# A conditioned transformer trunk: condition products in column strips, and the residual affine on GpSimd moved into the expert loop

## The reference, cut to what matters

```python
c_act = jax.nn.silu(c)
ada = c_act @ w_ada[l] + b_ada[l]                      # 1 x 6144
sh1, sc1, g1, sh2, sc2, g2 = jnp.split(ada, 6, axis=-1)
h = x * (1.0 + sc1) + sh1
m = pool mixer (layer 0) or sliding window attention (layer 1) of h
x = layernorm(ALPHA * x + g1 * m) * ln_g[l, 0] + ln_b[l, 0]
h = x * (1.0 + sc2) + sh2
f = moe(h)                                             # router, top 4, softmax, experts
x = layernorm(ALPHA * x + g2 * f) * ln_g[l, 1] + ln_b[l, 1]
```

## Time and profile before

| | us |
|---|---|
| median of three runs | 1534.92 |
| the profiled execution, its span | 1535.1 |
| end of the mixing in the head | 85.3 |
| last router feature of layer 0 made | 137.2 |
| last router product of layer 0 done | 146.5 |
| one expert block | 13.1 to 13.6 |

### The profile page before, as it was taken

One profiled execution on the slowest core, in us unless ns is written; L12 is line 12 of the kernel. 1 busy time (PEld: TensorE's weight loads), 2 busy tenths in 40 slices (PEclk: granted clock), 3 DMA queues, 4 the chain that ended last, 5 costly groups with the idle time before them and its releaser, 6 DMA issues.

```text
span 1535.1 us, 17763 instructions
## 1 busy us (share of the span) xinstructions
PE 1303.3 (85%) x4216; PEld 666.8 (43%) x4217; DVE 637.4 (42%) x1538; ACT 248.4 (16%) x565; POOL 489.0 (32%) x667
## 2 busy tenths in 40 slices
PE   7886688899889899986996887499989899888965
PEld 3545344444444444434544445244444444444422
DVE  0667125555555222259546766322222222122216
ACT  0111111111111111121113432111111111111111
POOL 0016533334443333323100025333333333333313
PEclk9987699999999999998996998599999999999987
DMA  9963579997897555562135504255746577566434
GB/s 359 360 246 137 223 266 351 350 355 282 313 344 277 218 191 207 181 230 104 61 137 193 196 1 189 77 200 196 266 181 234 211 296 270 191 250 258 158 117 164
DMA packets 92244, 339.22 MB, mean 221 GB/s; under 512 B 17321, under 2 KB 39593, under 8 KB 74674
## 3 DMA queue, kind: packets, MB, share of 16 engines
q1 hardware_dynamic: 50098, 284.23, 49.3%
q0 software_dynamic: 21312, 33.61, 6.0%
q10 hardware_dynamic: 20800, 20.97, 4.0%
HBM read 338.55 MB, written 44.04 MB: 249 GB/s over the span
## 4 chain that ended last, share of the span: by engine, by line
PE 64%; DVE 10%; issue 8%; POOL 5%; DMA 4%; SPq 4%; POOLq 2%; ACT 2%; DVEq 0%; ACTq 0%
PE ps L821 25%; PE ps L834 16%; PE ps L807 5%; POOL onehot L622 4%; PE ps L996 4%; PE ps L1054 2%; DMA ring<-in_w_ada 2%; PE ps L713 2%; PE ps L890 2%; DMA big<-y_rows 2%; SPq L382 1%; SPq L385 1%; PE ps L796 1%; PE ps L753 1%; DVE big L1342 1%
## 5 line engine op out<-in xcount | busy, mean ns | idle before, releaser
L821 PE MATMUL ps<-ring,work 128*128 x576 | 260.4, 606 | 34.8 <-SPq L427 33.6
L821 PE MATMUL ps<-ring,big 128*128 x576 | 255.7, 597 | 33.8 <-SPq L427 33.6
L834 PE MATMUL ps<-ring,work 128*128 x576 | 261.6, 597 | 2.0 <-ACT work L1143 2.0
L1478 DVE TENSOR_SCALAR work<-ps 128x256 f32<-128x256 f32 x72 | 30.6, 425 | 482.0 <-PE ps L821 482.0
L622 POOL TENSOR_SCALAR onehot<-cst,rank_now 128x128 bf16<-128x128 f32 x312 | 183.9, 602 | 16.4 <-POOL rank_now L616 16.4
L821 PEld LDWEIGHTS ps<-ring,work 128*128 128x128 f32 x576 | 108.9, 193 | 169.7 <-issue 169.3
L821 PEld LDWEIGHTS ps<-ring,big 128*128 128x128 f32 x576 | 107.2, 190 | 164.9 <-issue 164.5
L643 POOL COPY scatter_at<-scatter_ring 128x1 int32 (+1 forms) x72 | 14.1, 196 | 494.3 <-DVE work L1497 252.6
L834 PEld LDWEIGHTS ps<-ring,work 128*128 128x128 f32 x576 | 103.8, 190 | 107.0 <-issue 105.6
L1139 ACT ACTIVATE work<-work 128x256 f32<-128x256 f32 x72 | 30.0, 417 | 578.9 <-DVE work L1478 578.9
L713 PE MATMUL ps<-ring,c_sig 128*128 128x512 f32 x160 | 75.8, 634 | 16.1 <-DMA ring<-in_w_ada 15.3
(11 more groups left out here) (202 smaller groups left out, 1665.8 us busy)
## 6 DMA issues: line engine op xcount, KB each, us to landing
ring<-in_w_up SPq DMA_DIRECT2D x64, 2048.0 KB, 7.9
ring<-in_w_down SPq DMA_DIRECT2D x64, 1024.0 KB, 10.9
ring<-in_w_ada SPq DMA_DIRECT2D x18, 2048.0 KB, 14.5
big<-y_rows SPq DMA_DIRECT2D x8, 2048.0 KB, 7.9
big<-in_w_ada ACTq DMA_DIRECT2D x12, 1024.0 KB, 10.4
big<-in_w_kv_ada ACTq DMA_DIRECT2D x8, 1024.0 KB, 11.6
h_rows<-big SPq DMA_DIRECT2D x8, 512.0 KB, 6.9
ring<-in_w_q SPq DMA_DIRECT2D x2, 2048.0 KB, 10.6
```

Source lines behind the costliest of these rows:

```text
L821: mm = pe.matmul(U, xT[p][:, k, :], ring[:, bass.ds(at + k * UP, UP)], start=False, stop=(k == KC - 1))
L834: mm = pe.matmul(Y[:, h, :], aT[:, k, :], ring[:, bass.ds(at + k * D + h * HALF, HALF)], start=(k == 0), stop=(k == KF - 1))
```

## The change

All twelve pieces go over TensorE. A piece's eight matmuls now have a stationary operand of 32 columns and write to four strips of 32 partitions; strip j sums two of the eight products. VectorE takes the strips out of PSUM and adds a bias that has values in row 0 alone (`ada_part`), a ninth matmul with `strip_sel` (ones in rows 0, 32, 64 and 96) sums the four strips and spreads the sum to all partitions, and ScalarE copies it to `vec` (`ada_out`). The bias of layer 0 is loaded as one row of 24 KB, behind the first four pieces and x. The order of the pieces is changed, the pool weights come after four pieces instead of six, the mixer's features are made by halves of the columns, VectorE does the folding of the norm's parameters by halves, and `affine(0)` and `affine(2)` go into the first four expert blocks, one tile behind each block.

```diff
+ADA_ORDER = (2, 0, 3, 1, 4, 5, 8, 9, 6, 7, 10, 11)
+STRIP = 32
@@ SyncE
             for k in first[:2]:
                 load_static(k)
-            load_vectors([(0, 1), (0, 0)], P, s["vecs_landed"])
-            load_static(first[2])
             sp.dma_start(xres[:, :, :], x.rearrange("b (i p) d -> p (b i) d", p=P)).then_inc(s["x_landed"], 16)
-            load_static(first[3])
-            load_vectors([(0, 2), (0, 4)], P, s["gates_landed"])
+            for k in first[2:4]:
+                load_static(k)
+            sp.wait_ge(s["vec_cleared"], VEC)
+            sp.dma_start(vec[0:1, :, :].rearrange("p v d -> p (v d)"), b_ada[0:1, :]).then_inc(s["bias_landed"], 16)
 
             for k in first[4:7]:
                 load_static(k)
+            sp.dma_start(work[:, 1, :], pool_scale.to_broadcast([P, D])).then_inc(s["pscale_landed"], 16)
             sp.dma_start(cst[:, :], const).then_inc(s["const_landed"], 16)
...
-            load_vectors([(0, 5)], P, s["last_landed"])
@@ GpSimd, experts(l)
                 for b in range(PEELED):
                     body(b, b % 2)
+                    affine(2 * l, (b,))
@@ GpSimd, main
-            clear_vectors((3,))
+            clear_vectors(range(VEC))
             clear_rows(0)
-            prepare(0)
-            affine(0)
             experts(0)
...
             clear_rows(1)
-            affine(2)
             experts(1)
@@ TensorE
+            def ada(g):
+                key = ("ada", 0, ADA_ORDER[g])
+                w = slot_view(plan[key], KC * HALF)
+                wait_slot(pe, key)
+                if g >= 2:
+                    pe.wait_ge(s["part_ready"], g - 1)
+                for kk in range(2):
+                    for j in range(P // STRIP):
+                        k = 2 * j + kk
+                        mm = pe.matmul(ps[3][j * STRIP:(j + 1) * STRIP, g % 2, :],
+                                       c_sig[:, k:k + 1].to_broadcast([P, STRIP]),
+                                       w[:, k * HALF:(k + 1) * HALF], start=(kk == 0), stop=(kk == 1))
+                mm.then_inc(s["ada_mm"], 1)
+                pe.wait_ge(s["part_ready"], g + 1)
                 if g >= 2:
                     pe.wait_ge(s["ada_ready"], g - 1)
-                for k in range(KC):
-                    mm = pe.matmul(ps[3][:, g % 2, :], c_sig[:, k:k + 1].to_broadcast([P, P]),
-                                   w[:, k * HALF:(k + 1) * HALF], start=(k == 0), stop=(k == KC - 1))
+                pe.matmul(ps[2][:, g % 2, :], strip_sel[:, :], part[g % 2], start=True, stop=True
+                          ).then_inc(s["fold_mm"], 1)
@@ TensorE, main: pieces 0 to 3, pooling (four column groups after each half of the features),
@@ pieces 4 and 5, mixing, pieces 6 to 11, router
-            pe.wait_ge(s["hpool_ready"], TILES)
             for k in range(KC):
+                if k % 4 == 0:
+                    pe.wait_ge(s["hpool_ready"], TILES * (k // 4 + 1))
...
+            for g in range(4, 6):
+                ada(g)
             for i in range(TILES):
...
-            for c in on_pe[6:8]:
-                ada((0, c))
-            for n in range(H_FIRST):
-                pe.wait_ge(s["chunk_used"], n + 1)
-                spread(n, ps[3][:, n % 2, :], (s["ada_ready"], 8))
...
+            for g in range(6, len(ADA_ORDER)):
+                ada(g)
@@ ScalarE
+            def ada_out(g):
+                act.wait_ge(s["fold_mm"], g + 1)
+                if ADA_ORDER[g] // 2 in (1, 4):
+                    ins = act.activation(ada_cols(g), ps[2][:, g % 2, :], ACT.Identity, bias=one_col[:, :])
+                else:
+                    ins = act.activation(ada_cols(g), ps[2][:, g % 2, :], copy)
+                ins.then_inc(s["ada_ready"], 1)
@@ VectorE
+            def ada_part(g):
+                dve.wait_ge(s["ada_mm"], g + 1)
+                if g == 0:
+                    dve.wait_ge(s["bias_landed"], 16)
+                if g >= 2:
+                    dve.wait_ge(s["fold_mm"], g - 1)
+                dve.tensor_tensor(part[g % 2], ps[3][:, g % 2, :], ada_cols(g), ALU.add).then_inc(s["part_ready"], 1)
...
+            for g in range(3):
+                ada_part(g)
             dve.wait_ge(s["x_landed"], 16)
+            dve.wait_ge(s["ada_ready"], 2)
+            pool_features(0)
+            ada_part(3)
+            dve.wait_ge(s["const_landed"], 16)
+            step(dve.tensor_copy(bf_sel[:, :], cst[0:3 * NE, C_SEL:C_SEL + NE]))
...
             dve.wait_ge(s["ada_ready"], 4)
+            pool_features(1)
+            for g in range(4, 6):
+                ada_part(g)
...
-            chunk(("ada", 0, 6), 0, 1)
...
+            for i in range(3):
+                mixed(i)
+            ada_part(6)
+            ada_part(7)
+            mixed(3)
+            fuse_scale(0)
+            ada_part(8)
+            fuse_scale(1)
+            ada_part(9)
+            step(fuse_shift(0))
+            settle()
+            fuse_shift(1).then_inc(s["fused_ready"], 1)
             for i in range(TILES):
                 fused(0, i)
                 if i < 2:
-                    dve.wait_ge(s["last_landed"], 16)
-                    ada((0, 10 + i))
+                    ada_part(10 + i)
+            split_bup(0)
             route(0)
```

More of the change, by code:

```diff
@@ L114, in stream_plan @@
     plan, n = {}, 3
-    for c in range(12):
-        if c == 6:
+    for g, c in enumerate(ADA_ORDER):
+        if g == 4:
             plan[("pool", 0, 0)] = n
@@ L243, in build @@
         diag = ring[:, SLOT - TILES * (TOP - 1) * P:SLOT].rearrange("p (i k c) -> p i k c", i=TILES, k=TOP - 1)
+        part = [spare[:, at:at + HALF] for at in (512, 1024)]
         bd = spare[0:NE, 0:D]
@@ L311, in build, with ada_cols @@
         vec_flat = vec[:, :, :].rearrange("p v d -> p (v d)")
[L314 to L320, removed]
+        halves = [(v, h) for v in (0, 1, 2, 3, 4, 0, 1, 5) for h in range(2)]
+        plus_one = [n in (2, 3, 6, 7, 12, 13) for n in range(len(halves))]
+        H_LAST, H_ALL = 10, 16
+        def ada_cols(g):
+            slot, h = divmod(ADA_ORDER[g], 2)
+            return vec[:, slot, h * HALF:(h + 1) * HALF]
         used_up = {("pool", 0, 0): (s["poolmix_mm"], TILES), ("w_kv", 0, 0): (s["kv_mm"], TILES)}
@@ L440, in expert_loads @@
                         load_expert(l, e + RING, r)
+                late()
                 for r in range(RING):
@@ L895, in _ @@
             pe.wait_ge(s["c_act_ready"], 1)
-            for c in range(6):
-                ada((0, c))
+            pe.wait_ge(s["strip_ready"], 1)
+            for g in range(4):
+                ada(g)
             pool_n = plan[("pool", 0, 0)] % RING
@@ L940, in _ @@
             pe.wait_ge(m[0]["piece_added"], PIECES)
-            for n in range(H_FIRST, H_LAST):
-                spread(n, ps[3][:, n % 2, :], (s["bcast_done"], n - 1))
+            for n in range(H_LAST):
+                spread(n, ps[3][:, n % 2, :], (s["bcast_done"], n - 1) if n >= 2 else (s["ada_ready"], len(ADA_ORDER)))
             w_kv_at = slot_view(plan[("w_kv", 0, 0)], KC * KV)
@@ L1200, in _ @@
             act.activation(c_sig[:, :], c_col[:, :], ACT.Sigmoid).then_inc(s["sigmoid_ready"], 1)
+            def ada_out(g):
[5 more added lines that the diff above has]
+                ins.then_inc(s["ada_ready"], 1)
+            act.wait_ge(s["strip_ready"], 1)
+            for g in range(4):
+                ada_out(g)
             for k in range(KC):
@@ L1203, in _ @@
                 act.activation(pooled_t[:, k, :], ps[(k % 4) // 2][:, k % 2, :], copy).then_inc(s["pool_t_ready"], 1)
+            for g in range(4, 6):
+                ada_out(g)
             for i in range(TILES):
+                if i == 3:
+                    for g in range(6, 8):
+                        ada_out(g)
                 norm_std(0, i)
                 norm_apply(0, i)
+            for g in range(8, len(ADA_ORDER)):
+                ada_out(g)
             router(0)
```

135 lines of the change are left out of this document (58 added, 77 removed).

## The result

The changed kernel takes 1569.88 us (median of 4 runs, 1566.90 to 1570.87), the kernel before 1535.59 (4 runs, 1533.69 to 1536.91): ratio 1.0224, with a 95% interval of 1.0209 to 1.0239. It is 34 us slower; 1576 was forecast.

What follows compares the result with a forecast made beforehand. TensorE, busy in 85% of the span, with the head's chain going through whoever is late. 1535.1 + 6 (head) + 1 (block 0) + 23.6 (stalls) + 14.4 (clock) - 4 (layer 1) = 1576 us; range 1537 to 1602.

Steps and rivals of the forecast that it cites:

- The head: Start of the kernel up to layer 0's router: router's end moves from 146.5 to 152.3, 6 us later.
- rival A: Head products: four strips at once, a piece's records within 2 us; head -5, total 1565; chance 0.17 with both stall prices.
- The stalls and the clock: Expert blocks: affine delays the one-hot matrix, six TensorE stalls, 11.5 and 12.1 us; low clock behind them 14.4 us.
- The strips: Head products on TensorE: only neighbouring strips overlap, so a piece's records take 3.9 us.
- the order of the records: Head products: a float32 matmul's two records share a strip and follow each other, so only neighbours overlap: 3.9 us, not 1.9.
- the affine's departure from the features: Head: GpSimd's affine beside the features stretched a 1.22 us operation to 3.26; its removal counted within the new head's sum.
- The norm's loads: End of a layer: parameters are loaded 13 us or more before use, so their loading is hidden.
- The waits for the bias row and the constants: Head: first take-over waits for the bias until 33 us; VectorE waits for the constants until 59 us.
- The sum for the constants: Head loads: piece 5 at 51.5, piece 6 at 57 (2 MB in 5.4 us), then pool_scale and constants at 59.
- Layer 1's -4: Layer 1's features and router without the affine beside them: 2.9 us plus an estimated 1 us earlier, -4 us.
- the contention in block 0: Expert block 0: affine falls into the wait for the next gather, at most 1 us through VectorE.

Runs made afterwards that it cites:

- Experiment 1: Changed kernel with the residual affine in the four written-out blocks moved ahead of the scatter instead of behind it: 1536.26 us.
- experiment 4: Changed kernel with three needless TensorE products in front of the places of blocks 2 and 3, both layers: 1564.68 us.
- experiment 9: Changed kernel with affine ahead of scatter, norm loads and bias row from ScalarE, constants before pooling weights, and strip loops exchanged: 1516.35 us, one run.
- experiment 2: Kernel before with only the affine moved behind each block's scatter (blocks 0 to 3) and norm parameters loaded at the layer's end: 1560.48 us.
- experiment 10: Kernel before, its own head kept, with the affine in the blocks ahead of the scatter and norm loads issued from ScalarE: 1514.43 us.
- experiment 6: Changed kernel with the affine ahead of the scatter, norm loads from ScalarE, and the bias row loaded early from ScalarE's queue: 1528.49 us.
- experiment 7: As experiment 6, with the constants loaded ahead of the pooling weights: 1514.48 us.
- experiment 3: Changed kernel with condition products at full width, 128 columns, and only row 0 folded: 1601.31 us.

## Why the prediction was right, and where its steps were wrong

The direction and the mechanism of the loss came out, and the time lies within the range, 6 us from the forecast. The head did not come out: the prediction's own sign for rival A, the records of a piece ending within 2 us, was seen. A's total, 1565, is 5 us from the measured one. Step by step:

**The stalls and the clock held.** Forecast 11.5 and 12.1 us of stalls with 14.4 of clock, together 38.0; the stretches grew by 37.0. By the rows the stalls are 21.0, 2.6 smaller than I had them, and the clock 14.9, 2.5 a stall where I took 2.4; 1.1 is the rest. Experiment 1 shows that the affine's place causes all of it, experiment 4 that the clock is a part of its own. The Trainium skill (TensorE: Matmul & The Clock Gate, HAM oscillation) describes a kernel with waits of about 3 to 5 us, each of which leaves the products behind it at the low clock. The six stalls agree, the one of 2.44 us too, behind which the eight down products took 5.72 us instead of 3.60.

**The head was +6 and came out at -8, and two terms of it were mis-sized.** The strips: 3.9 us a piece by an overlap of two; 1.92 measured. Rival A, with four at once, had the mixing's end at 90 (measured 88.9), the last feature at 129.5 (130.6) and the router at 141 to 142 (138.1). The reason for which I ranked it lower, the order of the records, is refuted by experiment 9. The second term was the affine's departure from the features. I had seen one row at 3.26 us instead of 1.22 and took the new head's own sum as the answer; I never worked out what the old head would gain by the same move alone. It is 16.0 us in experiment 2 and 14.0 in experiment 10, 12 of them by the affine in both, the rest by the load and the clock ahead of the features. So the parts of the diff that rebuild the head cost about 8 us as it was built, with the bias and the constants late, and the one that only moves the affine out of it more than paid for them.

**The norm's loads were costed at nothing; they cost 2.7 us.** I asked when their data is needed (13 us later) and not what stands behind their issue on SyncE.

**The waits for the bias row and the constants were right**: take-over at 33 (31.5), constants at 59 (54.4). The sum for the constants has a slip: it takes 5.4 us for 2 MB "at x's pace", where its own 9.4 MB in 29.05 us give 6.5. Experiments 6 and 7 give their price in this head: 2.8 and 14.0 us, by the marks 3.3 and 13.3. Only in this order, though; the bias was waited for first, but the constants held the gain back.

**Layer 1's -4** was seen as -3.7 from its features on (its additions take 0.69 us again), and 2.4 of it was lost in the attention before them, which took 265.5 us at a mean granted clock of 0.88 instead of 263.1 at 0.89.

**The total** came nearer than its terms, and that is luck. The sum made the span 41 us longer and it is 30.0 longer: the head is off by -14.2, the contention in block 0 by -1, stalls and clock by -0.9, the norm's loads by +2.8, layer 1 by +2.7, the last stretch by -0.4. Between the medians the change is 34.3 us, so that the forecast is 6 off.

## What to carry to other kernels

A step moved into another engine's idle time has to be moved to where that idle time *is*: here the 9 us stood ahead of the scatter and the work was put behind it, one line further down, and that line is worth 34 us. Price a removal alone before pricing the change as a whole: what an operation costs its neighbours (two element-wise engines side by side) may be more than the new design earns (here 12 us of a head that the new design made 8 longer). And a load has two prices, when its data is needed and what its issue stands in front of.

## What the chip showed that I had not expected

- Four strips of 32 columns run at once with float32 operands too, 1.92 us for eight products over 512 columns instead of 7.03, in either order of the strips (experiments 3 and 9).
- Idle times of 2.4 to 4.7 us inside dense expert blocks were enough to bring the granted clock down, and three needless products of 2.74 us in all, which cost nothing, kept it up for the products that followed in the four stalls where they stood (experiment 4).
- GpSimd's affine beside VectorE's features slows VectorE up to 2.7 times (1.22 to 3.26 us) while its own operations take 2.35 us in the median and 3.32 at most; taken out of the head it gave about 12 us (experiments 2 and 10).
- A bias row of 24 KB, issued by SyncE at 20.08 us behind five transfers of 2 MB, was there at 31.5 us; issued by ScalarE at 6.19 it was there by 13.9 (experiment 6).
